# A gated linear attention layer's keys, squares and gate products put in another order, two of a delta layer's value tiles moved to another engine, and a forgetting attention's first score tiles in one float32 product

## The chip, the cores and the metric

One NeuronCore of a Trainium2 chip runs the whole program in one launch. The metric is the device time of one execution in microseconds. Engine names are those of the profile: PE is TensorE (PEld its weight loads), DVE VectorE, ACT ScalarE, POOL GpSimd, SP the queue that issues most DMAs.

## What is computed

A stack of eight layers on x of 512 tokens by 1024 features, all in float32: Fox (attention with a forget gate), GLA (gated linear attention), GDN (gated delta rule), Fox again, differential attention, feed-forward, short gated convolution, feed-forward. The change is in the first four. Their cores, shortened:

```python
# fox: per head, q and k rms-normalised, blocks of 128 query rows
logits = einsum('qd,kd->qk', qb, k) * dh ** -0.5 + (cum_q - cum_k)
p = softmax(where(pos_q >= pos_k, logits, -inf)); o = p @ v
y = (o * silu(z)) @ w_out

# gla: 4 heads, key dim 128, value dim 256, chunks of 64 tokens
q_dec = q * dk ** -0.5 * exp(bcum)
k_inv = k * exp(-bcum)
k_dec = k * exp(b_last - bcum)
o = where(causal, q_dec @ k_inv.T, 0) @ v + q_dec @ state     # then state = state * decay + k_dec.T @ v
o = rms_norm(o, o_gain);  y = (o * silu(z)) @ w_out

# gdn: 8 value heads; rows of values scaled by beta before the triangular solve
q, k = l2_norm(q), l2_norm(k);  vb = v * beta
```

## The kernel before

Each engine has one program written out by hand, and the programs meet at semaphores. A Python list `stages` gives the order: for each layer projections ("project"), the mixer ("fox", "gla", "gdn"), and a "join" (output projection, residual, norm of the next layer). Weights stream from HBM in panels of 1024 by 512: SP loads a half panel into a slot, ACT copies it into float32-replicated form (`weights_high`), POOL subtracts to get the rest (`weights_low`, L823), and PE forms each product from three passes, high by high, high by low, low by high (`three`, L900 to L902; L949 and L954 are the same in another order, all highs before the lows). PE's own program is strictly in order, so what it waits for stops everything behind it; pieces of the next projection ("gate pieces", chunks) are laid between the dependent steps of a mixer as filling.

**GLA front.** DVE evicts the last of four query and key tiles (L3000) and then, head by head, makes the decayed queries (L3397, into `buf_b[:, h]`), the keys grown by the inverse decay (L3399, `buf_b[:, 4 + h]`) and the decayed keys (L3403, into `buf_a`), and counts `gla["keys"]` once a head. PE has finished two gate pieces; it waits for four keys, transposes the decayed keys of four token tiles (L1648; two banks in turn, ACT copies each out at L2528), and then makes the scores inside chunks (`inside`, L1657). ACT's queue holds the two gates (`take_gate`, L2516) ahead of those copies.

**GLA end.** After the recurrence over eight chunks ACT copies the last token tile's output out (L2535), squares eight tiles of it (`square`, L2520) with gate 4 between them, DVE adds them in pairs (L3437), PE sums over partitions (L1702), DVE and ACT make the inverse root (`norm_rows`, L2700 to L2712; ACT's Ln and Exp in `inverse_root`, L2001 and L2002) and PE spreads it over the partitions (L1169). DVE multiplies the outputs by gain and gate (`scale_by_gate`, L3444: tiles 0 to 2 while ACT works on the root, 3 to 5 after the root), then by the spread root (L3457), ACT makes the high part (L1990) and DVE the low part (L2681). PE's join begins when two low parts stand; half of it (two of four token tiles) takes 48 matmuls of 128x512, and the second half waits for all eight gated tiles.

**GDN front.** PE turns value tiles (`turn_values`, L1735); DVE scales the first four of eight into rows (`first_values`, L3480) in the pause of `norm_rows`, ACT the last four (L2580). PE then waits for the root to spread it (`spread_norms`, L1169).

**Fox.** Eight heads of four row tiles. `scores(n)` for row tile i of head h is `three` over (i + 1) * 128 keys and one matmul with the forget sums (L1500). ACT makes the high parts of a head's queries and keys in one copy (`scores_high`, L2332), at the end of the head two before it; DVE makes the low parts in place (L3265). ACT also takes each turned tile (`take_turned`, L2347).

```python
norm_rows(st, bank[2], GLA_HEADS, 2 * P, RMS_EPS, n_squares=8, meanwhile=lambda: scale_by_gate(0, 1, 2))
scale_by_gate(3, 4, 5)
```

## Time and profile before

| | |
|---|---|
| median of 3 runs | 2364.1 us (2362.1 to 2365.77) |
| the profiled execution | 2361.91 us, of which the span is 2360.2 us |
| granted PE clock, mean of that execution | 0.995 |
| PE busy | 2289.7 us, 97% |
| DVE busy | 1282.4 us, 54% |
| ACT busy | 1020.1 us, 43% |
| POOL busy | 775.0 us, 33% |
| HBM | 187.84 MB read, 80 GB/s over the span |

One engine is nearly always busy, so a change elsewhere counts only as far as PE waited for it. The profiled execution is 2.2 us shorter than the median; times from its trace are on its own scale. Positions below are microseconds from the start of the span; the first Fox layer's scores lie around 130 to 250, the second's around 1120 to 1250, the GLA mixer from 405 to 492, the GDN front from 660 to 692.

### The profile page before, as it was taken

What the parts mean: (1) busy time and instruction counts of PE and PEld (TensorE: products, weight loads), DVE (VectorE), ACT (ScalarE), POOL (GpSimd) and SP (SyncE); (2) the same over time, 40 slices, a digit from 0 to 9 for tenths busy, and PEclk for the clock granted to TensorE, in tenths of its full rate; (3) what the DMA queues carried; (4) which work ended last, traced back from release to release, by engine and by line L of the source; (5) the groups of instructions that cost most, each with busy time, mean ns of one, the idle gap of its engine ahead of it and who ended that gap; (6) DMA issues with size and microseconds to landing.
All of it is one profiled execution on the core that took longest, in us unless ns stands there. A gap on an engine that the chain in (4) does not pass through costs nothing. (4 is left out here: it accounts for less than half of the span.)

```text
span 2360.2 us, 37346 instructions
## 1 busy us (share of the span) xinstructions
PE 2289.7 (97%) x14848; PEld 1954.7 (83%) x14848; DVE 1282.4 (54%) x2110; ACT 1020.1 (43%) x1690; POOL 775.0 (33%) x571
## 2 busy tenths in 40 slices
PE   9999999999999999999999989999999999999998
PEld 7877877878868878887887658999988888999986
DVE  6444246245635545544225774877754344777754
ACT  4345435143444543345434553554524323544522
POOL 3423344134420025333333413111254454111264
PEclk9999999999999999999999999999999999999999
DMA  5333222132210014432222212233223323233232
GB/s 153 72 72 72 82 90 89 36 81 77 89 54 3 3 38 98 90 72 54 83 89 72 72 37 72 90 107 107 93 105 106 107 89 108 90 108 107 89 107 89
DMA packets 137038, 191.96 MB, mean 81 GB/s; under 512 B 31024, under 2 KB 84656, under 8 KB 136896
## 3 DMA queue, kind: packets, MB, share of 16 engines
q1 hardware_dynamic: 128928, 183.64, 26.3%
q10 hardware_dynamic: 7968, 6.32, 0.9%
q8 instruction: 102, 1.67, 0.3%
q14 instruction: 40, 0.33, 0.0%
HBM read 187.84 MB, written 2.10 MB: 80 GB/s over the span
## 5 line engine op out<-in xcount | busy, mean ns | idle before, releaser
L823 POOL TENSOR_TENSOR weights_low<-weights_raw,weights_high 128x512 fp32r<-128x512 f32 x520 | 705.6, 1388 | 1205.6 <-ACT weights_high L1982 1205.6
L1982 ACT ACTIVATE weights_high<-weights_raw 128x1024 fp32r<-128x1024 f32 x260 | 260.9, 1050 | 384.3 <-PE bank L902 379.3
L900 PE MATMUL bank<-xt_high,weights_high 128*128 128x256 f32 (+1 forms) x1152 | 390.3, 339 | 3.9 <-ACT third_sum L2304 1.6
L902 PE MATMUL bank<-xt_high,weights_low 128*128 128x256 f32 (+1 forms) x1152 | 381.6, 331 | 0.0
L901 PE MATMUL bank<-xt_low,weights_high 128*128 128x256 f32 (+1 forms) x1152 | 381.0, 331 | 0.0
L900 PEld LDWEIGHTS bank<-xt_high,weights_high 128*128 128x128 f32 x1152 | 219.1, 190 | 30.7 <-POOL weights_low L823 4.9
L902 PEld LDWEIGHTS bank<-xt_high,weights_low 128*128 128x128 f32 x1152 | 218.9, 190 | 21.2
L901 PEld LDWEIGHTS bank<-xt_low,weights_high 128*128 128x128 f32 x1152 | 219.3, 190 | 16.6
L900 PE MATMUL bank<-weights_high,xt_high 128*128 128x512 f32 x432 | 173.7, 402 | 5.4 <-DVE xt_low L2869 2.8
L902 PE MATMUL bank<-weights_high,xt_low 128*128 128x512 f32 x432 | 168.8, 391 | 0.0
L901 PE MATMUL bank<-weights_low,xt_high 128*128 128x512 f32 x432 | 168.5, 390 | 0.0
L901 PE MATMUL bank<-token_sums,weights_high 128*128 128x256 f32 x576 | 163.0, 283 | 0.0
L900 PE MATMUL bank<-token_sums,weights_high 128*128 128x256 f32 x576 | 163.0, 283 | 0.0
L902 PE MATMUL bank<-token_sums,weights_low 128*128 128x256 f32 x576 | 163.0, 283 | 0.0
L847 POOL TENSOR_TENSOR weights_low<-weights_raw,weights_high 128x1024 fp32r<-128x1024 f32 x20 | 48.5, 2426 | 341.3 <-ACT weights_high L2235 341.3
L2882 DVE SCALAR_TENSOR_TENSOR x<-x,bank 128x512 f32<-128x512 f32 x64 | 41.7, 682 | 168.5 <-PE bank L902 146.6
L900 PE MATMUL bank<-weights_high,gated_high 128*128 128x512 f32 x288 | 114.0, 396 | 6.0 <-DVE gated_low L2681 4.2
L2235 ACT ACTIVATE weights_high<-scaled_after_mixer 128x1024 fp32r<-128x1024 f32 x80 | 84.6, 1058 | 66.7 <-PE bank L902 45.6
L902 PE MATMUL bank<-weights_high,gated_low 128*128 128x512 f32 x288 | 112.8, 392 | 0.0
L901 PE MATMUL bank<-weights_low,gated_high 128*128 128x512 f32 x288 | 112.7, 391 | 0.0
L901 PEld LDWEIGHTS bank<-token_sums,weights_high 128*128 128x128 f32 x576 | 110.6, 192 | 0.0
L902 PEld LDWEIGHTS bank<-token_sums,weights_low 128*128 128x128 f32 x576 | 110.6, 192 | 0.0
(487 smaller groups left out, 4860.6 us busy)
## 6 DMA issues: line engine op xcount, KB each, us to landing
weights_raw<-in_fox_w_in_dram SPq DMA_DIRECT2D x64, 512.0 KB, 5.6
weights_raw<-in_ffn_w_gate_dram SPq DMA_DIRECT2D x44, 512.0 KB, 4.0
weights_raw<-in_ffn_w_up_dram SPq DMA_DIRECT2D x44, 512.0 KB, 5.0
weights_raw<-in_ffn_w_down_dram SPq DMA_DIRECT2D x40, 512.0 KB, 4.3
weights_raw<-in_gla_w_in_dram SPq DMA_DIRECT2D x24, 512.0 KB, 4.3
weights_raw<-in_gdn_w_in_dram SPq DMA_DIRECT2D x24, 512.0 KB, 4.5
weights_raw<-in_attn_w_qkv_dram SPq DMA_DIRECT2D x24, 512.0 KB, 4.5
weights_raw<-in_conv_w_in_dram SPq DMA_DIRECT2D x24, 512.0 KB, 4.3
```

Of the source, the lines that this page charges most:

```text
L823: pool.tensor_tensor(w_lo[:, odd, k], raw[:, odd, k], w_hi[:, odd, k].bitcast(F32), ALU.subtract)\
L847: pool.tensor_tensor(ring_slot(w_lo, ring[name]), weights_of(name), ring_slot(w_hi, ring[name]).bitcast(F32), ALU.subtract).then_inc(up_lo ...
L900: pe.matmul(out_ap, lh, rh, start=first, stop=False, skip_group_check=skip)
L901: pe.matmul(out_ap, lh, rl, start=False, stop=False, skip_group_check=skip)
L902: return pe.matmul(out_ap, ll, rh, start=False, stop=last, skip_group_check=skip)
L1982: act.activation(w_hi[:, odd, 2 * m:2 * m + 2], raw[:, odd, 2 * m:2 * m + 2], ACT.Copy)\
L2235: act.activation(ring_slot(w_hi, ring[name]), weights_of(name), ACT.Copy).then_inc(w_high, 1)
L2882: dve.scalar_tensor_tensor(o, o, st["keep"], bank[2 * tt + j][:], ALU.mult, ALU.add)\
```

## The change

It has four parts. In the GLA front DVE makes both forms of the keys for all heads first and the queries after; PE waits for the queries before `inside(0)`. At the GLA end ACT takes gate 4 and squares tiles 0 to 5 of the first three token tiles before the last token tile is there, then the last token tile of those six in one instruction, then tiles 6 and 7; DVE gates tiles 0 and 1 before the row sums, 2 to 4 in the pause of the root, and 5 between the products with the root. In the GDN front ACT scales value tiles 2 and 3, and gates 3 and 4 come after them. In Fox, ACT copies a head's first 128 queries and keys in float32 to a tile of its own, and PE makes the first row tile's scores from it in one float32 product.

```diff
@@ Fox, PE
                         if i == 0:
                             pe.wait_ge(fox["q_taken"], 16 * nth + 8 + h + 1)
+                            pe.matmul(dst[:, 0:keys], first_rows_of[:, h % 2, 0], first_rows_of[:, h % 2, 1],
+                                      start=True, stop=False)
...
-                        three(dst[:, 0:keys], [v[:, i * P:i * P + P] for v in queries], [v[:, 0:keys] for v in operand], True, False)
+                        if i:
+                            three(dst[:, 0:keys], [v[:, i * P:i * P + P] for v in queries], [v[:, 0:keys] for v in operand],
+                                  True, False)
@@ GLA, PE
+                    pe.wait_ge(gla["keys"], 2 * GLA_HEADS)
                     inside(0)
@@ Fox, ACT
+                        act.activation(first_rows_of[:, h % 2], qk[:, :, h, 0:P], ACT.Copy)
                         act.activation(score_high(h)[:], qk[:, :, h], ACT.Copy).then_inc(fox["k_taken"], 1)
@@ GLA, ACT
+                        if tt == TT - 1:
+                            take_gate(4)
+                            act.wait_ge(gla["out_taken"], 2 * tt)
+                            act.wait_ge(gla["update"], 2 * (2 * tt - 1) + 2)
+                            for n in range(6):
+                                act.activation(buf_c[:, n, 0:tt * P], buf_a[:, n, 0:tt * P], ACT.Square)
...
-                    for n in range(2):
-                        square(n)
-                    take_gate(4)
-                    for n in range(2, 8):
+                    late = slice((TT - 1) * P, SEQ)
+                    act.activation(buf_c[:, 0:6, late], buf_a[:, 0:6, late], ACT.Square).then_inc(squares_done, 6)
+                    for n in range(6, 8):
                         square(n)
@@ GDN, ACT
-                    for n in (3, 4):
-                        take_gate(n)
-                    for n in range(4, 8):
+                    for n in range(2, 8):
+                        if n == 4:
+                            take_gate(3)
+                            take_gate(4)
@@ GLA, DVE
                     dve.wait_ge(w_used[1], st["pair"])
+                    dve.wait_ge(dve_freed, st["dve"])
                     for h in range(GLA_HEADS):
                         dve.wait_ge(gla["decays"], 2 * h + 2)
-                        link(dve.scalar_tensor_tensor(buf_b[:, h], buf_a[:, h], float(P) ** -.5, decayed[:, h],
-                                                      ALU.mult, ALU.mult))
...
+                    for h in range(GLA_HEADS):
+                        dve.scalar_tensor_tensor(buf_b[:, h], buf_a[:, h], float(P) ** -.5, decayed[:, h],
+                                                 ALU.mult, ALU.mult).then_inc(gla["keys"], 1)
...
-                    dve.wait_ge(gla["norm_sums"], 1)
...
-                    norm_rows(st, bank[2], GLA_HEADS, 2 * P, RMS_EPS, n_squares=8, meanwhile=lambda: scale_by_gate(0, 1, 2))
-                    scale_by_gate(3, 4, 5)
+                    scale_by_gate(0, 1)
+                    dve.wait_ge(gla["norm_sums"], 1)
+                    norm_rows(st, bank[2], GLA_HEADS, 2 * P, RMS_EPS, n_squares=8, meanwhile=lambda: scale_by_gate(2, 3, 4))
                     for n in range(8):
                         h = n // 2
+                        if n == 3:
+                            scale_by_gate(5)
@@ GDN, DVE
                     def first_values():
-                        for n in range(4):
+                        for n in range(2):
                             take_values(n)
```

DVE in the GLA front, from the last eviction on, before (B holds queries in its first half and grown keys in its second, A the projected queries and keys):

```order
L3000 COPY A<-bank 128x512 x4
L3397 SCALAR_TENSOR_TENSOR B<-A,decay 128x512
L3399 TENSOR_TENSOR B<-A,inverse_decay 128x512
L3403 TENSOR_TENSOR A<-B,decay 128x512
L3397 SCALAR_TENSOR_TENSOR B<-A,decay 128x512
L3399 TENSOR_TENSOR B<-A,inverse_decay 128x512
L3403 TENSOR_TENSOR A<-B,decay 128x512
```

and with the change:

```order
L3013 COPY A<-bank 128x512 x4
L3411 TENSOR_TENSOR B<-A,inverse_decay 128x512
L3415 TENSOR_TENSOR A<-B,decay 128x512
L3411 TENSOR_TENSOR B<-A,inverse_decay 128x512
L3415 TENSOR_TENSOR A<-B,decay 128x512
L3411 TENSOR_TENSOR B<-A,inverse_decay 128x512
L3415 TENSOR_TENSOR A<-B,decay 128x512
L3411 TENSOR_TENSOR B<-A,inverse_decay 128x512
L3415 TENSOR_TENSOR A<-B,decay 128x512
L3418 SCALAR_TENSOR_TENSOR B<-A,decay 128x512 x4
```

Eight instructions instead of twelve stand before the last decayed key tile; the four for the queries follow it.

DVE at the GLA end, from the row sums to the first two low parts, before (A are the outputs, D the gates):

```order
L2700 TENSOR_SCALAR gla_mean_squares<-bank 4x512
L2702 MEMSET gla_factors_high_and_low 128x512
L3444 SCALAR_TENSOR_TENSOR A<-A,columns,D 128x512 x3
L2685 TENSOR_TENSOR gla_newton<-gla_reciprocals 4x512
L2686 SCALAR_TENSOR_TENSOR gla_newton<-gla_newton,gla_mean_squares 4x512
L2687 SCALAR_TENSOR_TENSOR gla_reciprocals<-gla_newton,gla_reciprocals 4x512
L2711 CAST gla_factors_high_and_low<-gla_reciprocals 4x512
L2712 TENSOR_TENSOR gla_factors_high_and_low<-gla_reciprocals,gla_factors_high_and_low 4x512
L3444 SCALAR_TENSOR_TENSOR A<-A,columns,D 128x512 x3
L3457 TENSOR_TENSOR gla_gated<-A,bank 128x512
L3457 TENSOR_TENSOR gla_gated_second<-A,bank 128x512
L2681 TENSOR_TENSOR gated_low<-gla_gated,gated_high 128x512
```

and with the change, from the root's last steps on:

```order
L2724 CAST gla_factors_high_and_low<-gla_reciprocals 4x512
L2725 TENSOR_TENSOR gla_factors_high_and_low<-gla_reciprocals,gla_factors_high_and_low 4x512
L3474 TENSOR_TENSOR gla_gated<-A,bank 128x512
L3474 TENSOR_TENSOR gla_gated_second<-A,bank 128x512
L2694 TENSOR_TENSOR gated_low<-gla_gated,gated_high 128x512
L3474 TENSOR_TENSOR gla_gated<-A,bank 128x512
L2694 TENSOR_TENSOR gated_low<-gla_gated_second,gated_high 128x512
L3458 SCALAR_TENSOR_TENSOR A<-A,columns,D 128x512
```

Nothing stands any more between the root's last step and the first product; the gate product of tile 5 comes after the second low part, and two of the others now stand ahead of the row sums.

## Rows read from the trace of the kernel before

**Rows 1.** The page, busy time by engine (us, share of the span, instructions).

```profile
PE 2289.7 (97%) x14848; PEld 1954.7 (83%) x14848; DVE 1282.4 (54%) x2110; ACT 1020.1 (43%) x1690; POOL 775.0 (33%) x571
```

**Rows 2.** Waits of PE, 400 to 500 us: waiter, releaser, us in total, times, longest.

```profile
PE bank L900 <- DVE gated_low L2681: 3.7, 1, 3.7
PE bank L1648 <- DVE A L3403: 2.3, 1, 2.3
```

**Rows 3.** Waits of PE, 660 to 700 us.

```profile
PE bank L1169 <- DVE gdn_factors_high_and_low L2712: 1.4, 1, 1.4
```

**Rows 4.** Waits of PE, 100 to 260 us.

```profile
PE bank L900 <- POOL weights_low L823: 0.7, 2, 0.5
```

**Rows 5.** Timeline of PE, 392 to 421 us: start us, us, engine, line, operation, tiles, shapes, xcount, [idle before].

```profile
408.64 1.98 PE L954 MATMUL bank<-xt_high,weights_low 128*128 128x512 f32 x8
...
415.22 2.01 PE L1657 MATMUL bank<-B 128*128 128x128 f32 x16
```

**Rows 6.** Timeline of DVE, same stretch.

```profile
401.11 1.74 DVE L3399 TENSOR_TENSOR B<-A,inverse_decay 128x512 f32<-128x512 f32 x1
...
412.08 0.69 DVE L3403 TENSOR_TENSOR A<-B,decay 128x512 f32<-128x512 f32 x1
```

**Rows 7.** Timeline of POOL and then of ACT, same stretch.

```profile
401.00 6.39 POOL L823 TENSOR_TENSOR weights_low<-weights_raw,weights_high 128x512 fp32r<-128x512 f32 x4 [3.34 <-ACT weights_high L1982]
...
410.43 1.08 ACT L2516 ACTIVATE D<-bank 128x512 f32<-128x512 f32 x2 [7.26 <-PE bank L954]
...
413.59 1.09 ACT L2528 ACTIVATE keys_decayed_rows<-bank 128x512 f32<-128x512 f32 x2 [2.07 <-PE bank L1648]
```

**Rows 8.** Timeline of ACT, then PE, from 470 us.

```profile
471.68 0.60 ACT L2535 ACTIVATE A<-bank 128x512 f32<-128x512 f32 x1 [13.52 <-PE bank L1683]
...
475.28 1.02 PE L1702 MATMUL bank<-C,column_pick 128*4 128x512 f32 x2
...
479.75 0.50 PE L900 MATMUL bank<-xt_high,weights_high 128*128 128x512 f32 x1
...
488.05 1.07 PE L1169 MATMUL bank<-gla_factors_high_and_low,row_pair_selector 128*128 128x512 f32 x4
...
666.06 7.12 PE L1163 MATMUL bank<-gdn_squares,column_pick 128*8 128x512 f32 x16
```

**Rows 9.** Timeline of DVE, 470 to 500 us.

```profile
481.12 2.33 DVE L3444 SCALAR_TENSOR_TENSOR A<-A,columns,D 128x512 f32<-128x512 f32 x3
...
486.78 5.21 DVE L3444 SCALAR_TENSOR_TENSOR A<-A,columns,D 128x512 f32<-128x512 f32 x3
...
494.84 0.69 DVE L2681 TENSOR_TENSOR gated_low<-gla_gated_second,gated_high 128x512 fp32r<-128x512 f32 x1
```

**Rows 10.** Timeline of POOL, 470 to 500 us.

```profile
486.74 6.38 POOL L823 TENSOR_TENSOR weights_low<-weights_raw,weights_high 128x512 fp32r<-128x512 f32 x4 [33.07 <-ACT weights_high L1982]
```

**Rows 11.** Busy time by stretch: bounds, us, each engine's busy us (x), PE clock, DMA share, GB/s.

```profile
497.00:500.40 3.40, 3.40 (x10) 2.62 (x9) 2.44 (x3) 2.00 (x4) 3.40 (x3) 0.50 0.09 36
...
542.80:548.20 5.40, 3.14 (x15) 3.12 (x15) 2.62 (x7) 4.87 (x9) 4.75 (x4) 0.68 0.57 178
```

**Rows 12.** Timeline of DVE and then of ACT, 662 to 700 us.

```profile
678.66 0.67 DVE L2685 TENSOR_TENSOR gdn_newton<-gdn_reciprocals 8x512 f32<-8x512 f32 x1
...
677.25 0.63 ACT L2002 ACTIVATE gdn_reciprocals<-gdn_reciprocals 8x512 f32<-8x512 f32 x1
...
683.72 4.66 ACT L2580 ACTIVATE C<-bank,gate_columns 128x128 f32<-128x128 f32 x16 [2.51 <-PE bank L1735]
```

**Rows 13.** Timeline of PE's weight loads: Fox scores of a first row tile, then full float32 products.

```profile
166.61 0.19 PEld L901 LDWEIGHTS bank<-queries_and_keys_low,ueries_and_keys_high 128*128 128x128 f32 x1
...
166.72 0.19 PEld L902 LDWEIGHTS bank<-ueries_and_keys_high,queries_and_keys_low 128*128 128x128 f32 x1
...
415.11 1.93 PEld L1657 LDWEIGHTS bank<-B 128*128 128x128 f32 x16
```

**Rows 14.** Timeline of ACT, 168 to 174 us.

```profile
171.94 0.60 ACT L2347 ACTIVATE fox_probs_transposed<-bank 128x512 f32<-128x512 f32 x1 [1.17 <-PE bank L1509]
```

1 line of the change is left out of this document (added).

## The prediction, made before the changed kernel was run

> **What bounds the kernel now.** Start with busy time by engine: PE is busy for 2289.7 of 2360.2 us [rows 1]. No other engine comes near it, so the change can pay in two ways alone: PE gets less work, or a stretch in which PE stands idle gets shorter. The table of waits, asked for PE in the stretches that the edits touch, says which idle stretches there are. In the GLA mixer they are 3.7 us before the join, behind a low part of DVE, and 2.3 us before the key transposes, behind the last decayed key tile [rows 2]. At the GDN front 1.4 us end with the root's factors [rows 3]. In a Fox layer's scores PE waits 0.7 us in all, and for POOL [rows 4]: an edit of ACT or DVE has nothing to win there, only the matmuls themselves have. All these times are of the profiled execution, which took 2361.91 us; the median of the three runs is 2364.1, so 2.2 us are added at the end.
>
> **1. Keys first (GLA front).** PE's last pass of the gate pieces starts at 408.64 and takes 1.98, so PE is free at 410.62; the scores inside chunks start in the weight queue at 415.11 [rows 5, 13]. Those 4.49 us hold 16 transposes and the waits. DVE's last decayed key tile starts at 412.08 and takes 0.69 [rows 6]. Now 8 instructions lead up to it and not 12. Which four fall away matters: while POOL runs, 401.00 to 407.39, each of DVE's takes 1.7, afterwards 0.69 [rows 6, 7]. The contended time stays full, so the four saved are cheap ones: 4 x 0.7 = 2.8 us, minus 0.1 for the added wait on DVE's own eviction. The last key tile ends at 412.77 - 2.7 = 410.1, before PE is free: the 2.3 us go. What is late next is ACT: its queue has two gates from 410.43 to 411.51, and only then the copies of the transposed keys, which started at 413.59 before [rows 7]. PE can't run on past two token tiles without them. So the chain from ACT's first copy to the scores, 415.11 - 413.59 = 1.52, starts at 411.5: scores at 413.0. The four query products end at 410.1 + 4 x 0.65 = 412.7, just in time for the new wait. Gain 2.1 us; bounds: 2.3 (all of the wait) and 1.0 (if the queries were slowed to 0.9 each and more by something I don't see).
>
> **2. Squares early (GLA end).** Six squares of 384 columns and gate 4 are put on ACT while it is idle: before the last token tile's output copy it waited 13.52 us for PE, and seven instructions of at most 0.60 are 4.2, at no cost unless that idle time went. After the two output copies comes one square of 6 x 128 columns, taken as 0.8 us, a half more columns than the 0.60 of one of 512 [rows 8]. DVE's sums are then ahead of PE, which does its four row sums back to back. Before, they ran from 475.28 to the next piece at 479.75, 4.47 us; eight unhindered ones of the same width take 7.12, or 0.89 each [rows 8], so four take 3.56. Gain 0.9 us; bounds 0.3 (ACT's two last squares come as late for the fourth sum as all did before) and 1.2 (the pause ahead of the first falls away too).
>
> **3. Gate products spread (GLA end).** This is the largest term. Today DVE does three gate products between the root's factors and the first product with the root, 5.21 us because POOL runs from 486.74 to 493.12; in the pause three took 2.33 [rows 9, 10]. With the edit two stand ahead of the row sums, three in the pause, and the sixth after the second low part. The factors are ready as early as before (less part 2), at 485.9; the spread matmuls follow PE's pieces at 488.05 - 0.9 = 487.15 [rows 8]. From there: the first product at 487.6 once the first spread is through, two products to 488.8, ACT's second high part about 489.3, the first low part, in POOL's time, 1.5 (between 0.69 and 1.74) to 490.8, a product to 491.4, the second low part 0.7 to 492.2. Before, the second low part ended at 495.53 [rows 9], and PE's join began then. 495.53 - 492.2 = 3.3, of which 0.9 are part 2: gain 2.4 us, and 1.3 of the wait are left. Bounds: 1.2, if both low parts are slowed, and 3.3, if neither waits for anything.
>
> The Trainium skill, SBUF — State Buffer, section Who interferes with whom, says that a DVE instruction with two SBUF inputs is shut out for as long as a POOL instruction that reads SBUF runs, while one with an input from PSUM is not. That fits the products with the root against the gate products. By it the first low part could wait a whole POOL instruction (6.38 / 4 = 1.6) and then take its own 0.69, and this term would be 1.6 instead of 2.4.
>
> **The clock.** After PE's 3.75 us of idleness the granted clock was 0.50 of full (1.2 instead of 2.4 GHz) from 497.0 to 500.4 [rows 11]: 3.4 us in which half the work was done, so 1.7 us lost. A shorter wait can do the same: of the 5.4 us from 542.8 PE was busy 3.1, and the mean clock was under full [rows 11]. Behind the 2.3 us at 410.6 nothing of the kind is seen: the weight loads of the scores stand 0.12 apart [rows 13]. So the outcome is open around 2.3 us, and I take the remaining 1.3 for short enough: gain 1.7; the other bound is 0. DVE's chain then becomes close. The join's second half waits for all eight gated tiles. PE reaches it 48 passes after 492.2, 10.8 us at a quarter of a row sum's 0.89 each, at 503.0; DVE has 12 instructions left, 8 of 0.7 and 4 of 1.4 in POOL's next run, 11.2 less overlaps, 503.1 or so. So 0.1 is taken back: gain 1.6.
>
> **4. GDN front.** DVE ended its fourth value tile and began the root's steps at 678.66, though ACT's exponential had ended at 677.88 [rows 12]. With two tiles fewer it begins at 677.95: gain 0.7 of the 1.4 us. ACT takes the two tiles behind the exponential: 16 pieces took 4.66, so 8 take 2.3, to 680.2, then a table load and two gates, taken as 2.5 us, by 682.7. ACT's next piece waited for PE until 683.72 [rows 12], now 683.0: still covered, by 0.3. Bounds 0.4 and 1.4.
>
> **5. Fox, one float32 product.** A first row tile's passes stand 0.11 apart in the weight queue, three are 0.34. A full float32 product of the same size is two records, and eight of them take 1.93: 0.24 each [rows 13]. 2 layers x 8 heads x 0.095 = 1.5 us. Against it: 16 ACT copies of 256 columns, 0.38 each by estimate from the 0.60 of one of 512, all in front of a high part. Where ACT comes to the next turned tile it had idled 1.17 us [rows 14], so the delay is used up before anyone waits. Bounds for the matmuls: 16 x 0.11 = 1.8, and -0.9, which is the rival E below.
>
> Nothing changes in the instructions of POOL or SP, and no DMA is added. Weight loads stand well ahead of PE in these stretches, so a PE that runs earlier doesn't meet them. **Sum:** 2.1 + 0.9 + 2.4 + 1.6 + 0.7 + 1.5 = 9.2 us. 2361.9 - 9.2 = 2352.7 on the scale of the trace, 2354.9 on that of the median: **2355.0 us**.
>
> **The rivals.**
> A, the forecast, 2355.0.
> B, the clock falls after the remaining wait all the same: 1.6 are not won, 2356.6. For it: of two waits of 2.3 us one was followed by a slow stretch and one was not, so length alone doesn't settle it.
> C, POOL slows both low parts and the clock falls as well: 1.2 + 1.6 less, 2357.8. For it: POOL's run starts with the same PE piece as before, so it moves along with the chain, and the second low part begins where I let POOL end.
> D, a second gain of the clock: the 2.3 us wait at the GLA front is cut to 0.7, and in other executions it may have cost a slow stretch, or a later idle stretch is spared one: 1.7 more, 2353.3.
> E, full float32 is slower. A row sum of 512 columns takes 0.89 us [rows 8], a quarter of that is 0.22 for 512 columns or 0.056 for 128. If the columns set the pace and full float32 goes over them four times, a tile costs 0.22 where three replicated passes cost 0.17: 16 x 0.056 = 0.9 lost instead of 1.5 won, 2357.4. The Trainium skill, FP8 and Floating Point Precision, section TensorE Precision Notes, says the same: true float32 is four passes through the array. Against it: the weight queue's rows, by which a pass of 128 columns costs 0.11 and not 0.057 [rows 13].
> F, slower than before. ACT's copy stands ahead of the high part, the next exponentials, the turned tiles and the weights' high parts. If ACT's idle time were not free but part of the loop of DVE's maximum, ACT's exponential and PE's transposes, each copy would show in full, 16 x 0.38 = 6.1, and again at the weights' high parts that POOL's low parts wait for, up to 6.1: 12.2 - 9.2 = 3.0 over, 2367. It decides once ACT's idle time before a turned tile is under 0.38; rows 14 have 1.17.
> G, the waits only move: PE meets the queries at the GLA front, and the join's second half meets DVE. Half of parts 1, 3 and the clock, 3.1 us, and the GDN term are lost with 0.9 of the Fox term: 4.7 less, 2359.7.
>
> **How the numbers follow.** Chances: A 0.48, B 0.14, C 0.10, D 0.10, E 0.07, F 0.04, G 0.07. A measurement of this kernel tells about 0.2%, 4.7 us, from no change, so faster is below 2359.4: A to E, 0.89, from which I take 0.04 for part costs missed together; 0.85. Slower means above 2368.8, which only half of F reaches, with some more lost beside it: 0.02. The rest, 0.13, lies within 0.2%. The range runs from 2351.0, D with the upper bounds of parts 1 to 3, to 2359.5, just short of G.
>
> **What would show it.** In the trace of the changed kernel: at the GLA front a PE wait on ACT's key copies of about 0.7 us and none on DVE, scores about 2.4 us after the last gate piece instead of 4.5; four row sums 0.9 apart; a wait of about 1.3 us before the join and a granted clock of full speed behind it; 0.7 us before the GDN spread; 16 matmul records fewer in all (two for three); in the Fox scores a first tile's product as two records 0.12 apart and PE waits there as before, 0.7 a layer. I am wrong if the wait before the join is over 2 us, if the clock halves there, if PE waits on DVE in the join's middle for more than 0.5 us, or if PE's waits in a Fox layer pass 2 us.

## The result, and the profile after

| | before | changed | ratio, 95% interval |
|---|---|---|---|
| median of 6 and 6 runs, us | 2364.64 (2362.1 to 2366.74) | 2351.14 (2350.24 to 2352.11) | 0.9944 [0.9933, 0.9954] |
| again, beside the variants below, 9 and 5 runs | 2364.87 (2362.52 to 2366.92) | 2353.89 (2352.28 to 2354.47) | 0.9952 [0.9939, 0.9966] |
| profiled execution (span) | 2361.91 (2360.2) | 2350.92 (2349.2) | |

The changed kernel is faster, by 13.5 us in the first comparison and 11.0 in the second; 9.1 were forecast (2364.1 to 2355.0). The profiled executions differ by 11.0, where the terms add up to 9.2. The predicted range, 2351.0 to 2359.5, holds both medians, the first one barely. What has to be explained is that the terms came out within 0.5 us of the forecast each and that the time fell by 2 to 4 us more than their sum.

**Busy time by engine of the changed kernel, from the page** (us, share of the span, instructions), against [rows 1]:

```profile
PE 2284.1 (97%) x14832; PEld 1950.6 (83%) x14832; DVE 1279.7 (54%) x2108; ACT 1028.0 (44%) x1715; POOL 775.2 (33%) x571
```

PE has 16 records fewer, as forecast (two for three, 16 times), and 5.6 us less busy time. ACT has 25 more instructions and 8 us more.

**Waits of PE in the changed kernel, 392 to 493 us** (waiter, releaser, us in total, times, longest), against [rows 2]:

```profile
PE bank L901 <- DVE gated_low L2694: 1.0, 1, 1.0
PE bank L1653 <- ACT keys_decayed_rows L2535: 0.6, 1, 0.6
```

The 3.7 us before the join are 1.0, and the 2.3 us on DVE's last key tile are gone. What is late next at the front is ACT's copy of the turned keys, as forecast (0.7).

**Timeline of the changed kernel at the GLA front: PE, DVE, POOL, then ACT** (start us, us, engine, line, operation, tiles, shapes, xcount, [idle before <-releaser]), against [rows 5 to 7]:

```profile
407.64 1.98 PE L955 MATMUL bank<-xt_high,weights_low 128*128 128x512 f32 x8
...
412.04 2.01 PE L1662 MATMUL bank<-B 128*128 128x128 f32 x16
```

```profile
405.28 1.78 DVE L3411 TENSOR_TENSOR B<-A,inverse_decay 128x512 f32<-128x512 f32 x1
...
408.42 0.69 DVE L3415 TENSOR_TENSOR A<-B,decay 128x512 f32<-128x512 f32 x1
409.03 2.49 DVE L3418 SCALAR_TENSOR_TENSOR B<-A,decay 128x512 f32<-128x512 f32 x4
```

```profile
400.00 6.51 POOL L824 TENSOR_TENSOR weights_low<-weights_raw,weights_high 128x512 fp32r<-128x512 f32 x4 [3.29 <-ACT weights_high L1988]
```

```profile
409.43 1.09 ACT L2523 ACTIVATE D<-bank 128x512 f32<-128x512 f32 x2 [7.26 <-PE bank L955]
410.40 1.09 ACT L2535 ACTIVATE keys_decayed_rows<-bank 128x512 f32<-128x512 f32 x2
```

The last gate pass starts 1.00 us earlier than before (0.53 from the first Fox layer's scores, the rest at places that fox_alone names below, and spread), the scores inside chunks 3.18 us earlier: 2.18 us are won here. The scores stand 2.4 us behind the end of the gate pieces (409.62 to 412.04), which is the number in the forecast. The last key tile ends at 409.11, before PE is free, and the four query products, at 0.62 each and outside of POOL's run, end at 411.52, half a microsecond before PE asks for them.

**Timeline at the GLA end: PE, ACT, DVE, POOL**, against [rows 8 to 10]:

```profile
472.11 3.60 PE L1708 MATMUL bank<-C,column_pick 128*4 128x512 f32 x8
...
483.97 1.07 PE L1170 MATMUL bank<-gla_factors_high_and_low,row_pair_selector 128*128 128x512 f32 x4
```

```profile
459.76 2.57 ACT L2545 ACTIVATE C<-A 128x384 f32<-128x384 f32 x6
468.50 0.60 ACT L2548 ACTIVATE A<-bank 128x512 f32<-128x512 f32 x1 [6.17 <-PE bank L1689]
...
470.08 0.85 ACT L2556 ACTIVATE C<-A 128x768 f32<-128x768 f32 x1
```

```profile
473.45 1.53 DVE L3458 SCALAR_TENSOR_TENSOR A<-A,columns,D 128x512 f32<-128x512 f32 x2
...
477.06 2.33 DVE L3458 SCALAR_TENSOR_TENSOR A<-A,columns,D 128x512 f32<-128x512 f32 x3
...
486.00 1.02 DVE L2694 TENSOR_TENSOR gated_low<-gla_gated,gated_high 128x512 fp32r<-128x512 f32 x1 [0.32 <-ACT gated_high L1996]
487.15 0.69 DVE L3474 TENSOR_TENSOR gla_gated<-A,bank 128x512 f32<-128x512 f32 x1
487.76 0.95 DVE L2694 TENSOR_TENSOR gated_low<-gla_gated_second,gated_high 128x512 fp32r<-128x512 f32 x1
```

```profile
482.67 5.50 POOL L824 TENSOR_TENSOR weights_low<-weights_raw,weights_high 128x512 fp32r<-128x512 f32 x4 [32.16 <-ACT weights_high L1988]
```

The last two of those four POOL instructions, one by one:

```profile
485.18 1.30 POOL L824 TENSOR_TENSOR weights_low<-weights_raw,weights_high 128x512 fp32r<-128x512 f32 x1
486.43 1.74 POOL L824 TENSOR_TENSOR weights_low<-weights_raw,weights_high 128x512 fp32r<-128x512 f32 x1
```

The four row sums (two records each) take 3.60 us in one row instead of being spread over 4.47; the six early squares are fitted into ACT's idle time, of which 6.17 us are still left. At the spread the gain has grown from 3.17 to 4.08 us: 0.91 for the squares. The join starts at 488.77 instead of 495.58, 6.81 us earlier: 2.73 for the gate products. Both low parts began while a POOL instruction ran, and took 1.02 and 0.95, neither the free 0.69 nor the 1.74 of [rows 6]. The single rows say why: POOL's instructions end at 486.48 and 488.17, the low parts at 487.02 and 488.71, each 0.54 us later. What a low part loses is what is left of the POOL instruction that it meets.

**Busy time by stretch** (bounds, us, each engine's busy us (x), PE clock, DMA share, GB/s), against [rows 11]: the join's first pieces of the changed kernel, and two stretches further on.

```profile
488.70:492.10 3.40, 3.33 (x15) 2.76 (x16) 3.23 (x5) 2.71 (x4) 2.57 (x2) 1.00 0.67 264
537.40:540.80 3.40, 3.40 (x18) 3.40 (x17) 1.30 (x8) 2.03 (x6) 3.40 (x3) 0.50 0.78 287
1380.50:1387.30 6.80, 3.82 (x17) 2.81 (x17) 4.42 (x13) 4.08 (x11) 0.36 (x1) 0.50 0.46 157
```

PE has full clock behind the join's start: 15 instructions in the stretch where before had 10. Matched instruction by instruction, the lead grows there from 6.81 to 8.45 us: 1.64 for the clock (1.6 forecast). The two other stretches at 1.2 GHz have counterparts in before, at 544.8 and 1391.3.

**Waits of PE at the GDN front, 655 to 700 us**, against [rows 3], and ACT's timeline there, against [rows 12]:

```profile
PE bank L1170 <- DVE gdn_factors_high_and_low L2725: 0.8, 1, 0.8
```

```profile
668.89 0.63 ACT L2008 ACTIVATE gdn_reciprocals<-gdn_reciprocals 8x512 f32<-8x512 f32 x1
669.43 2.27 ACT L2593 ACTIVATE C<-bank,gate_columns 128x128 f32<-128x128 f32 x8
671.72 1.28 ACT L2573 ACT_TABLE_LOAD   x1
673.01 1.09 ACT L2573 ACTIVATE D<-bank 128x512 f32<-128x512 f32 x2
674.72 3.50 ACT L2593 ACTIVATE C<-bank,gate_columns 128x128 f32<-128x128 f32 x12 [0.62 <-PE bank L1741]
```

The wait is 0.8 instead of 1.4 (1.39 and 0.78, so 0.6 us are won), and ACT is ready 0.62 us before the next turned values come: what it took over is covered.

**Weight loads of a first row tile's scores in the first Fox layer: before (the first pass and the load behind the third, on both sides of [rows 13]), then the changed kernel**, and ACT's copies in it (line, engine, names, shapes, xcount, busy us, mean ns, idle before):

```profile
166.38 0.19 PEld L900 LDWEIGHTS bank<-ueries_and_keys_high 128*128 128x128 f32 x1
...
166.83 0.19 PEld L1500 LDWEIGHTS bank<-cumulated_high_and_low,row_pair_selector 128*128 128x128 f32 x1
```

```profile
165.98 0.42 PEld L1498 LDWEIGHTS bank<-first_queries_and_keys 128*128 128x128 f32 x2
166.32 0.19 PEld L1505 LDWEIGHTS bank<-cumulated_high_and_low,row_pair_selector 128*128 128x128 f32 x1
```

```profile
L2338 ACT ACTIVATE first_queries_and_keys<-queries_and_keys 128x256 f32<-128x256 f32 x8 | 3.3, 407 | 0.1
```

From the first load to that of the forget sums it was 0.45 us and is 0.34. Over a whole layer less than this 0.11 per product shows, as fox_alone tells below. (The second Fox layer's scores lie from 1024 to 1138 in before, not from 1120 to 1250 as was said above.)

### The profile page after: what moved, and what is told of

Its sections match the earlier page's. It is cut to its first block and busy times, and to the rows that moved or that the text cites. A ratio compares the mean times of both kernels' runs of the same rounds, so it can differ in the third digit from the quotient of the medians.

```text
span 2349.2 us, 37341 instructions
## 1 busy us (share of the span) xinstructions
PE 2284.1 (97%) x14832; PEld 1950.6 (83%) x14832; DVE 1279.7 (54%) x2108; ACT 1028.0 (44%) x1715; POOL 775.2 (33%) x571
## 3 DMA queue, kind: packets, MB, share of 16 engines
q8 instruction: 102, 1.67, 0.3%
## 5 line engine op out<-in xcount | busy, mean ns | idle before, releaser
L901 PEld LDWEIGHTS bank<-token_sums,weights_high 128*128 128x128 f32 x576 | 110.6, 192 | 0.0
L902 PEld LDWEIGHTS bank<-token_sums,weights_high 128*128 128x128 f32 x576 | 110.6, 192 | 0.0
```

The costliest lines, as they stand in the source:

```text
L901: pe.matmul(out_ap, lh, rh, start=first, stop=False, skip_group_check=skip)
L902: pe.matmul(out_ap, lh, rl, start=False, stop=False, skip_group_check=skip)
```

## The experiments

All of them are timed beside before on the same chip, and matched instruction by instruction with its trace. "Lead" is how much earlier a place of PE's program is reached than in the trace of before.

**The three GLA edits, one at a time.** Each kernel is before with one part of the diff.

```diff
@@ keys_alone
+pe.wait_ge(gla["keys"], 2 * GLA_HEADS)
+dve.wait_ge(dve_freed, st["dve"])
-        link(dve.scalar_tensor_tensor(buf_b[:, h], buf_a[:, h], float(P) ** -.5, decayed[:, h],
-                                      ALU.mult, ALU.mult))
...
+    for h in range(GLA_HEADS):
+        dve.scalar_tensor_tensor(buf_b[:, h], buf_a[:, h], float(P) ** -.5, decayed[:, h],
+                                 ALU.mult, ALU.mult).then_inc(gla["keys"], 1)
```

> Before plus the keys-first edit alone. Theory 1 (the parts add, and the clock's share hangs on the wait before the GLA join): the scores inside chunks start 2.2 us earlier after the gate pieces (3.4 instead of 4.5 to 6.6 us behind them; before 415.22 less 408.64, after 412.04 less 407.64), every later place moves by that amount and no more, the wait before the join stays 3.7 us and the half-clock stretch behind it stays. Time 2.2 us under before, ratio 0.9991. Rival (the wait of 2.3 us at this front costs before a slow stretch of the clock in executions that were not profiled, which would explain that the medians differ by 13.5 us and the profiled executions by 11.0): 2.2 plus up to 1.7, so 3 to 4 us, ratio 0.9983 to 0.9987.

2360.83 us against 2364.22: ratio 0.9988 [0.9980, 0.9997], 3.4 us. In the trace the wait on DVE is gone and the one on ACT is 0.6; the lead grows by about 2.2 us at this front. (From the start of the last gate pass to the scores it is 4.4 us instead of 6.6; the 3.4 of the expectation doesn't follow from its own positions.) PE still waits 3.7 before the join, with a clock of 0.50 behind it:

```profile
492.40:499.20 6.80, 5.64 (x13) 4.46 (x14) 5.66 (x8) 4.51 (x7) 4.61 (x4) 0.50 0.38 145
```

This stretch begins within the wait and lasts 6.8 us, where that of before begins 1.4 us behind the join's start and lasts 3.4; over it keys_alone loses 1.0 of its 2.2 us. The whole profiled execution is only 1.3 us shorter than before's, while the medians are 3.4 apart. They show 1.2 us more than the gain at the front, which leans to the rival; the interval (0.7 to 4.7 us) holds both.

```diff
@@ squares_alone (ACT)
+if tt == TT - 1:
+    take_gate(4)
+    act.wait_ge(gla["out_taken"], 2 * tt)
+    act.wait_ge(gla["update"], 2 * (2 * tt - 1) + 2)
+    for n in range(6):
+        act.activation(buf_c[:, n, 0:tt * P], buf_a[:, n, 0:tt * P], ACT.Square)
...
-for n in range(2):
-    square(n)
-take_gate(4)
-for n in range(2, 8):
+late = slice((TT - 1) * P, SEQ)
+act.activation(buf_c[:, 0:6, late], buf_a[:, 0:6, late], ACT.Square).then_inc(squares_done, 6)
+for n in range(6, 8):
     square(n)
```

> Before plus the early squares alone. Theory 1: the four row sums take 3.60 instead of 4.47 us, so 0.9 us by the GLA spread; the wait before the join and the half clock behind it stay, time 0.9 us under before, ratio 0.9996. Rival (the products of the gate need the room too): with the sums earlier but DVE's three gate products still ahead of the first product with the root, the wait before the join grows by part of the 0.9, and the gain is 0 to 0.5.

2362.88 us, ratio 0.9995 [0.9987, 1.0004]: not told from no change by itself. In the trace the row sums take 3.60 us in one row, 0.94 are won, and the wait before the join is 3.7 as before: the rival, that it grows, is out. This execution had a stretch that before's has not, behind the 2.3 us wait:

```profile
413.20:416.60 3.40, 3.38 (x16) 3.02 (x17) 0.00 (x0) 1.65 (x3) 0.00 (x0) 0.50 0.02 5
```

```diff
@@ gates_alone (DVE)
-dve.wait_ge(gla["norm_sums"], 1)
-norm_rows(st, bank[2], GLA_HEADS, 2 * P, RMS_EPS, n_squares=8, meanwhile=lambda: scale_by_gate(0, 1, 2))
-scale_by_gate(3, 4, 5)
+scale_by_gate(0, 1)
+dve.wait_ge(gla["norm_sums"], 1)
+norm_rows(st, bank[2], GLA_HEADS, 2 * P, RMS_EPS, n_squares=8, meanwhile=lambda: scale_by_gate(2, 3, 4))
 for n in range(8):
+    if n == 3:
+        scale_by_gate(5)
```

> Before plus the spread gate products alone. Theory 1: the wait before the join falls from 3.75 to about 1.0 us (2.7 won) and the half-clock stretch at 497.0 goes with it (1.6 to 1.7 more): 4.3 us, ratio 0.9982. Rival (the clock follows what PE did over a longer time and not this one wait; the early squares or the keys are needed too): 2.7 us alone, ratio 0.9989, with a granted clock of 0.50 still seen behind the join's start. Second rival (without the early squares the two gate products ahead of the row sums delay DVE's sums): 0.7 less of either.

2359.90 us, ratio 0.9983 [0.9975, 0.9992], 4.3 us. Its waits of PE, 400 to 500 us, then the two stretches behind them:

```profile
PE bank L1648 <- DVE A L3403: 2.3, 1, 2.3
PE bank L900 <- DVE gated_low L2681: 1.2, 1, 1.2
```

```profile
415.20:418.60 3.40, 3.40 (x18) 3.40 (x18) 0.00 (x0) 1.44 (x3) 0.00 (x0) 0.50 0.02 5
...
495.40:498.80 3.40, 3.40 (x15) 2.83 (x16) 3.23 (x5) 2.64 (x4) 2.63 (x2) 1.00 0.79 271
```

The wait before the join falls to 1.2 and the clock behind it is full: 2.5 us and 1.6 us of lead, with the 2.3 us wait and a half clock behind it still there. So the clock behind the join's start hangs on the wait just before it, and the early squares aren't needed for that. Again the 2.3 us wait was followed by a stretch at half clock, which cost 1.5 us.

**The clock by itself.** Before, with matmuls whose results nobody reads in PE's two GLA waits; the other work and its order are unchanged.

```diff
@@ fill_waits (PE)
+for _ in range(34):               # a helper, keep_clock, written out
+    pe.matmul(bank[7][:, 0:P], ident_b[:], mask_b[:], start=True, stop=True)
 pe.wait_ge(gla["keys"], GLA_HEADS)
@@ before the first piece of the GLA join
+for _ in range(54):
+    pe.matmul(bank[2][:, 0:P], ident_b[:], mask_b[:], start=True, stop=True)
```

> Before with matmuls whose results nobody reads in PE's two idle waits of the GLA mixer: 34 of 128 columns ahead of the first key transpose (2.3 us of wait) and 54 ahead of the join (3.7 us of wait). The real work and its order are unchanged, so nothing of parts 1 to 3 is won; only the clock can change. Theory 1 (idleness of PE brings the half clock): the stretch of granted clock 0.50 at 497.0 goes, 1.6 us are won in the profiled execution, and if executions of before that were not profiled have a further slow stretch behind the 2.3 us wait, 2 to 3 us by the medians; ratio 0.9988 to 0.9993. Rival (the clock is not what made the join's first pieces slow, or it halves for a reason that lies outside these waits): no change, ratio 1.000, or slower by up to 0.5 us where the last extra matmul runs past the end of a wait.

2361.66 us, ratio 0.9992 [0.9984, 1.0001], 2.6 us. At the join's first piece the lead has not changed since 395 us (0.67), and eight pieces later it is 2.29: 1.6 us from the clock alone. The stretch in question:

```profile
495.40:498.80 3.40, 3.40 (x16) 2.76 (x16) 2.51 (x4) 2.91 (x5) 2.88 (x3) 1.00 0.40 159
```

**The three together.**

> Before plus the three edits of the GLA mixer together (keys first, early squares, spread gate products). Alone they gave 3.4, 1.3 and 4.3 us by the medians, 9.0 in sum, each with about 2 us of uncertainty. Theory 1 (the waits add: 2.2 + 0.9 + 2.7, and with the waits before the key transposes and before the join both short no half clock follows either of them, in any execution): positions in the trace earlier by 5.8 us at the join's start, 7.4 to 7.5 behind its first pieces; medians 9 to 11.5 us under before, ratio 0.9955 to 0.9962. Rival (each edit's gain is partly the same idle time, given once): 6 us or less, ratio 0.9975 or more. Second rival (the excess of the medians over the profiled executions sits in the Fox and GDN edits): 8 us, and gdn_alone with fox_alone at 5 us.

2355.67 us (6 runs) against 2363.84: ratio 0.9968 [0.9956, 0.9980], 8.2 us. The lead, counted from 395 us, is 5.8 us at the join's start and 7.5 behind its first pieces: 5.8 and 7.4 to 7.5 were expected, so in the trace the parts add. By the medians it is under the 9 to 11.5 of the first theory and over the rival's 6; alone the three gave 9.0. The second rival's 8 us came, but not its other half, since gdn_alone and fox_alone (below) give 1.7 us together and not 5. That the medians gain more from the three together than the trace does isn't shown.

**GDN and Fox.**

```diff
@@ gdn_alone (ACT, DVE)
-for n in (3, 4):
-    take_gate(n)
-for n in range(4, 8):
+for n in range(2, 8):
+    if n == 4:
+        take_gate(3)
+        take_gate(4)
@@ first_values
-for n in range(4):
+for n in range(2):
```

> Before plus the edit at the GDN front alone (two of DVE's value tiles go to ACT). Theory 1 (the parts add): PE's wait before the spread of the root's factors falls from 1.4 to 0.8 us, so 0.6 to 0.7 us are won there and stay to the end, ratio 0.9997, not told from no change by the medians. Rival (ACT's later gates delay something in the recurrence that follows): the gain is gone by the first solve step, or a new wait of PE on ACT over 0.5 us stands behind it, and the time is that of before or above.

2363.79 us against 2363.84, ratio 0.9998 [0.9989, 1.0008]. The wait falls from 1.4 to 0.8 and 0.6 us are won there; no new wait on ACT follows (its waits behind the spread are the same as those of before to a tenth). This execution too had the half clock behind the 2.3 us wait, at 415.3, and lost 1.5 us by it.

```diff
@@ fox_alone (PE; ACT has the copy of fox_copies)
+pe.matmul(dst[:, 0:keys], first_rows_of[:, h % 2, 0], first_rows_of[:, h % 2, 1], start=True, stop=False)
+if i:
     three(dst[:, 0:keys], [v[:, i * P:i * P + P] for v in queries], [v[:, 0:keys] for v in operand], True, False)
@@ fox_copies (ACT alone)
+act.activation(first_rows_of[:, h % 2], qk[:, :, h, 0:P], ACT.Copy)
```

> Before plus the Fox edit alone (one float32 product for a first row tile, and ACT's 16 copies). Theory 1: 16 fewer matmul records, 1.1 to 1.5 us won over the two layers in the trace, ratio 0.9994. Rival (the changed kernel's medians are 13.5 us better while its profiled execution is 11.0 better because the Fox layers win more in executions that are not profiled, for instance by the clock): 3 us or more in the medians, ratio 0.9987 or less. Second rival (full float32 sets the pace by its columns): 0.9 us slower, ratio 1.0004.

2362.24 us, ratio 0.9993 [0.9984, 1.0002], 1.6 us. The lead grows by 0.53 over the scores of either Fox layer: 1.06 us, 0.07 per product. Matched product by product, a product in the first layer brings 0.11, as in the weight queue, or 0.9 in eight, and 0.35 are given back at three pieces of a projection that stand between the scores. At two of them it is POOL's low part that PE's weight load then waits for, longer than before (in before the profile names no wait at the first and 0.45 us at the second):

```profile
150.09 0.19 PEld L901 LDWEIGHTS bank<-xt_high,weights_high 128*128 128x128 f32 x1 [0.24 <-POOL weights_low L824]
...
220.11 0.19 PEld L901 LDWEIGHTS bank<-xt_high,weights_high 128*128 128x128 f32 x1 [0.55 <-POOL weights_low L824]
```

The first rival, 3 us or more, finds nothing for it.

> Before plus ACT's 16 copies of the first rows of queries and keys alone; nobody reads them, the scores stay in three passes. Theory 1 (ACT's idle time before a turned tile covers a copy of 0.4 us): PE's waits in a Fox layer's scores stay at 0.7 us, the time is that of before, ratio 1.000. Rival (about a fifth of the expected Fox gain is missing in the trace because the copies are seen): 0.2 to 0.4 us slower at the places where a first tile's scores follow, and the trace shows PE waiting on ACT's high part there. Second rival (the copies are exposed in full): 16 x 0.4 = 6.4 us slower, ratio 1.0027.

2364.09 us, ratio 1.0003 [0.9994, 1.0012]. Waits of PE, 100 to 260 us, in fox_copies (fox_alone has the same row):

```profile
PE bank L901 <- POOL weights_low L824: 0.7, 2, 0.5
```

The lead does not move over either layer's scores. The copies, 0.41 us each, are wholly covered, and what is missing from the Fox term is not theirs. Behind the first layer, at 361.7, the lead grows by 0.28, in all seven kernels with the copies and in none of the six variants without; why isn't shown.

**The changed kernel again, and its largest remaining wait.** Behind a wait of 5.1 us in the differential attention the clock was at half in every trace. One variant fills the wait, one reorders the work around it, the last does both.

```diff
@@ attn_filled (PE, turn_pair)
-pe.wait_ge(diff["mixed"], n + 1)
 if n:
     pe.wait_ge(diff["turned_used"], n)
+if n == 25:
+    for _ in range(80):
+        pe.matmul(bank[6][:, 0:P], ident_b[:], mask_b[:], start=True, stop=True)
+pe.wait_ge(diff["mixed"], n + 1)
@@ attn_order (PE; then DVE)
+if n == DEEP - 1:
+    pair_scores(n + 3)
 turn_pair(n)
...
-if n < DEEP:
+if n < DEEP - 1:
     pair_max(n + 1)
-if n == DEEP - 1:
-    pair_max(n + 2)
 mix(n)
-if DEEP <= n < n_all - 2:
+if n == DEEP - 2:
+    pair_max(n + 2)
+if DEEP - 1 <= n < n_all - 2:
     pair_max(n + 2)
@@ order_filled (PE, on top of attn_order)
 if n == DEEP - 1:
+    pe.wait_ge(diff["turned_used"], n)
+    for _ in range(44):
+        pe.matmul(bank[6][:, 0:P], ident_b[:], mask_b[:], start=True, stop=True)
     pair_scores(n + 3)
```

In attn_order the sum of head 4's squares is moved from pair 24 to pair 26 as well.

> The changed kernel once more, beside the two variants below and on the same chip. Its medians were 13.5 us under before (6 executions each) where the five parts alone or in groups gave 8.2 (the three GLA edits together), 0.05 (GDN) and 1.6 (Fox), 9.8 in sum. Theory 1 (the parts add, and the rest is the spread of half-clock stretches over executions: the clock behind the wait before the GDN pieces, at 858 and behind the key transposes falls in some executions and not in others): 11 to 13 us, ratio 0.9945 to 0.9953. Rival (the Fox or the GDN edit is worth more in the presence of the others): 13 us or more again, ratio 0.9944 or less.

2353.89 us against 2364.87, 11.0 us: the lower edge of the first theory's range, and 2.5 us less than the first comparison gave. Its profiled execution took 2353.89 us, 3.0 more than the other one of the same program. Busy time by stretch of the two, the first of the first profile, the second of this one:

```profile
848.40:855.20 6.80, 5.63 (x45) 4.83 (x45) 4.44 (x9) 3.62 (x8) 0.00 (x0) 1.00 0.01 2
```

```profile
848.40:855.20 6.80, 6.43 (x30) 5.77 (x31) 2.27 (x5) 1.54 (x3) 0.00 (x0) 0.50 0.01 2
```

In the same 6.8 us the one gets through 45 instructions of PE and the other through 30. The second execution falls back by 2.3 us over this place.

> The changed kernel plus 80 matmuls of 128 columns whose results nobody reads, in PE's wait of 5.1 us in the attention (ahead of the transposes of the 26th pair of probabilities), into the bank that those transposes fill. The granted clock was 0.50 for 6.8 us behind this wait in all ten traces so far. Theory 1 (the wait brings the half clock and the pieces behind it are set by PE): the stretch goes and 1 to 2 us are won against the changed kernel. Rival (DVE sets the pace there, PE's slower clock is hidden): the stretch goes and the time stays within 0.3 us.

> The changed kernel with another order at the same place: PE issues the scores of pair 28 (counted from 0) ahead of the transposes of pair 25; DVE takes the maximum of pair 26 before the last rotation instead of behind it, mixes pair 25 before the maximum of pair 27, and sums head 4's squares two pairs later. Theory 1 (DVE's queue is what PE waits for): the transposes of pair 25 start about 2 us earlier (1381.5 instead of 1383.5), pair 28's scores 4 us earlier, and the layer ends 1 to 2 us earlier. Rival (DVE's total work up to the last pair is the same, so only the order of the waits changes): the 5.1 us shrink, and as much comes back before the last pairs; time within 0.5 us. If the wait is under 3 us, the half clock may go too, for up to 1 us more.

2352.43 and 2351.80 us, ratios 0.9951 [0.9937, 0.9964] and 0.9947 [0.9934, 0.9961] to before; the medians don't tell them from the changed kernel. By the traces, counted over this place alone: filled, the stretch at half clock goes and 0.6 us are won; reordered, the wait is 2.9 us, the half clock stays, and 0.7 us are won. Both first theories were too high, and DVE does set most of the pace here. The filled kernel's trace has something more, 30 us further on, in the layer's output projection:

```profile
1419.60:1423.00 3.40, 3.40 (x10) 2.62 (x9) 0.00 (x0) 0.00 (x0) 0.00 (x0) 0.50 0.00 0
```

PE waits 1.83 us there in all 14 traces, and this is the only one with the clock at half behind it. It costs 1.6 us, more than the filling had won: from 1425 on attn_filled has lost 1.1 us against the changed kernel's first profile. Whether the filling has to do with it isn't shown; order_filled, which fills as well, has no such stretch.

> The order of attn_order and, in the wait of 2.9 us that is left there before pair 28's scores, 44 matmuls of 128 columns whose results nobody reads. Theory 1 (order and clock are two gains): behind this place 0.7 to 0.9 us from the order, as attn_order showed in its trace, and 0.4 to 0.6 us from the clock, as attn_filled showed, 1.1 to 1.5 us under the changed kernel in the trace of this stretch; no half clock from 1378 to 1388. By the medians 2350 to 2352, ratio to before 0.9940 to 0.9948. Rival (DVE sets the pace from the 26th pair on once the order is right, so PE's clock no longer matters there): 0.7 us, as with the order alone.

2351.27 us against 2363.64: ratio 0.9949 [0.9936, 0.9963]. Busy time by stretch of attn_order, then of order_filled:

```profile
1379.80:1386.60 6.80, 4.81 (x21) 3.32 (x21) 5.95 (x16) 3.69 (x11) 0.00 (x0) 0.50 0.41 154
```

```profile
1380.50:1387.30 6.80, 4.81 (x37) 3.22 (x33) 6.29 (x18) 3.92 (x12) 0.00 (x0) 1.00 0.44 155
```

Against the changed kernel's first profile the lead grows from 0.2 to 2.0 us over this place, and 0.4 of it are gone again by 1500: 1.4 stay, within what was expected; the rival (0.7) is out. This is the version with the shortest profiled span of all, 2347.5 us, but 1.4 us are 0.06% and the medians can't confirm it against the changed kernel.

**The stretches at half clock in all 14 traces.** Each place is named by the wait of PE just before it. Every trace also ends at half clock, in its last 5 to 9 us, which the table leaves out.

| place | wait of PE | traces with the wait | of them with half clock behind |
|---|---|---|---|
| GLA key transposes, 410 | 2.3 | 6 | 3 |
| same, 0.6 or filled | 0.6 or less | 8 | 0 |
| GLA join, 490 | 3.75 | 6 | 6 |
| same | 1.2 or less, or filled | 8 | 0 |
| first GDN pieces, 534 to 546 | 2.25 | 9 | 3 |
| same | 1.57 to 1.67 | 5 | 0 |
| attention, 1380 | 5.1 | 11 | 11 |
| same, reordered | 2.9 | 1 | 1 |
| same, filled | 0.5 or 0.6 | 2 | 0 |
| attention's output projection, 1415 to 1432 | 1.83 | 14 | 1 (attn_filled) |
| GDN recurrence's end, 848 to 860 | several, 0.7 at most | 14 | 9 |

The front's 2.3 us wait brought a stretch in squares_alone, gates_alone and gdn_alone, and none in before, fox_alone and fox_copies. Without it, in eight traces, there was none. At the join the stretch lasted 3.4 us in before and fox_copies and 6.8 us in the other four, which lost 0.9 to 1.2 us more by it than before did.

## Why the prediction was right, and where its size was off

**Parts 1 to 4 held.** On profiled time, with before's trace as the other side: keys first 2.18 (2.1), squares 0.91 (0.9), gate products 2.73 (2.4), clock behind the join 1.64 (1.6), GDN front 0.6 (0.7). What was to be late next was late next: ACT's key copies by 0.56 (0.7) and a wait before the join of 1.0 (1.3). DVE was not late in the join's middle, for which 0.1 had been taken back.

**Gate products, 0.3 too low.** I took 1.5 for the first low part and 0.7 for the second; they took 1.02 and 0.95, each 0.3 over the free 0.69, because each met a POOL instruction near its end: 0.48 us of one were left and 0.41 of the next. In the GLA mixer of all 14 traces (395 to 505 us) 125 of DVE's instructions with two inputs from SBUF (keys, gate products, low parts) began while POOL's subtraction ran, and every one of them ended 0.54 or 0.55 us after the POOL instruction that it met. So the 1.5 was a guess between two prices, where the price follows from when DVE comes. The rule of the Trainium skill (SBUF — State Buffer, section Who interferes with whom) agrees with this: it has such an instruction shut out until POOL's is over. The prediction's 1.6 for this term took a whole POOL instruction of waiting; the actual rest of one was a third of that. The products with the root, which have an input from PSUM, took 0.69 beside the same run, and there too the trace agrees with the page.

**Fox, 0.4 too high.** The price, "0.24 each" against 0.34, or 0.095 per product, was about right: the weight queue and the leads at the products have 0.11. What was left out is that PE then meets POOL's low parts earlier and waits for them, which takes four tenths of it back: 1.06 us over both layers instead of 1.5, while the copies cost nothing. Rival E, four times the columns' price, is out: it had a loss of 0.9, and the product's two weight loads hold the queue for 0.34 us where three passes held it for 0.45. The Trainium skill's statement that true float32 is four passes through the array (FP8 and Floating Point Precision, section TensorE Precision Notes) may hold inside a record, which no run here shows; but the loss that rival E drew from it doesn't show at 128 columns, where each product gained what the weight queue gained, 0.11.

**The sum on the trace: 9.2 against 10.99.** Of the difference 1.5 us are one stretch at half clock that before's trace has (at 858.8) and the changed one's has not. It stands in 9 of the 14 traces and no part of the change touches it, so this is the spread of executions; the rest of the traces' difference is 9.5. The second profile of the changed kernel, which has such a stretch twice as long, lies 8.0 us under before's. 9.2 is between.

**The step that failed** is the one from the trace to the median: "2.2 us are added at the end", on both sides. Before's profiled execution is a good one: of the 81 executions of it that were timed beside the variants, 56 had a mean granted clock of 0.994 with a median of 2364.5 us, 16 had 0.995 (2362.9) and 9 had 0.996 (2361.6), and only 8 took no longer than the profiled one, which had 0.995. The changed kernel's first profile lies 0.2 us under its median, the second on it. So about 2 us of the gain are in executions that no profile of before shows.

The traces of the variants, which have before's program at these places, show where they may lie. One part is rival D's: behind the 2.3 us wait at the GLA front three of six kernels lost 1.2 to 1.6 us to the clock, none of the eight without the wait did, so an average execution of before loses some 0.7 us there (3 in 6, times 1.4). Rival D had 0.10 and should have been part of the forecast beside A, because the two don't exclude each other. A second part is as large: at the join's start before's profile has the short stretch at half clock, and four of the six kernels with the 3.7 us wait lost 0.9 to 1.2 us more there, 0.7 on average, so the term of 1.6 was read from a mild case.

A third part stands at 303, ahead of all GLA edits. There DVE's normalising product (two inputs from SBUF) and POOL's subtraction begin within 0.1 us of each other, and one of them is held up: in nine traces, before's and all seven with the Fox copies among them, POOL's takes 2.39 us instead of 1.28 and PE waits for nothing; in the other five DVE's takes 2.41 instead of 1.28, and PE loses 0.7 us. Five of the seven kernels without the copies had it, some 0.5 us on average. On the other side the stretch at 858.8, which before's profile has, costs its average execution about 0.5 less. What these three add, net about 1.4 us, is an estimate from one trace of each kernel.

keys_alone, 3.4 us by its medians and 2.2 by its trace, points the same way and doesn't prove it. What is left of the step from 11.0 to 13.5 us stays open; the two comparisons of the same pair differ by 2.5 us themselves.

**The range held the first comparison by a slip.** Its lower end is said to be rival D with the upper bounds of parts 1 to 3, which is 2353.3 less 0.2, 0.3 and 0.9, so 2351.9 and not 2351.0. The first median, 2351.14, lies under that; the second, 2353.89, over it. That the first is inside the stated range is luck.

Of rival C half came: POOL's run slowed both low parts, but by 0.3 each and not by 1, and the clock did not fall. B, F and G didn't come: the clock is full behind the remaining wait, the copies are covered, and no wait of PE took the place of those removed beyond the 0.56 and 1.0 that the sum had.

## What to carry to other kernels

When a wait of PE ends, two things are won: its length, and whatever clock was lost behind it. Read the granted clock just behind each long wait in more than one profile, because a wait may bring the half clock in one execution and not in the next, and one profile then under- or overstates what its removal is worth. If only the clock is at stake, matmuls with no reader in the wait can show it in one run, as at the join; look through the rest of that trace too, because in attn_filled what the filling won was lost again 30 us later. And count the price of a moved instruction at the place where it is moved to: the gate products that left POOL's run cost 0.8 and not 1.7, and a low part that meets POOL costs the rest of the POOL instruction and 0.54 us.

## What was not expected of the hardware

- Waits of 2.3 us were followed by a granted clock of 0.50 in 6 of 15 cases (two places), waits of 2.9 us and more in 18 of 18, waits of 1.7 us or less at the same four places in none of 23, and a wait of 1.83 us at a fifth place in 1 of 14. No other wait of 1.2 us or more in any trace was. At the end of the GDN recurrence, where PE has many waits of at most 0.7 us, it fell in 9 of 14.
- A stretch at half clock isn't always paid in full. The one in the first GDN pieces (before, at 544.8) cost 1.4 us at once against keys_alone, which has none there, and 1.1 of them came back 5 us behind its end: keys_alone waits 0.9 there for the next normalised rows, and before doesn't wait.
- Beside POOL's subtraction, DVE's instructions with two inputs from SBUF took anything from 0.95 to 1.83 us instead of 0.69 to 0.75, and yet there is one rule in it: in 125 of 125 cases in the GLA mixer they ended 0.54 or 0.55 us after the POOL instruction during which they began. In a row of both, DVE comes soon after the start of each POOL instruction and pays 1.66 to 1.83; in the changed kernel the low parts before the join and in its first pieces came later in it, and paid 0.95 to 1.36. POOL pays as well: its instruction that follows while DVE's runs takes 1.74 instead of 1.30. DVE's instructions with one input from PSUM took 0.69 beside the same POOL instructions.
